# Opening of a transformer-like layer: scale and shift groups loaded by column quarters

## The chip, the cores and the metric

The kernel runs on one core of a Trainium2 chip. The metric is the device time of one execution in microseconds. The engines are TensorE (PE), VectorE (DVE), ScalarE (ACT), GpSimd (POOL) and SyncE (SP), which only issues DMAs here; ACT issues some too.

## The reference

One layer on 512 latent tokens and 256 context tokens of width 1024, all in fp32. A condition vector (c for the latents, c_ctx for the context) gives nine vectors of 1024 through one linear map, `ada_w` of 1024 x 9216: shift, scale and gate of three sub-layers. The opening computes groups 0 (shift) and 1 (scale) of these and the first sub-layer's h:

```python
ml = jnp.split((jax.nn.silu(c) @ ada_w[i] + ada_b[i])[:, None, :], N_MOD, axis=-1)
h = rms_norm(t, norm_g) * (1 + scale) + shift
x = t + gate * (0.5 * (silu(h @ w_gate) * (h @ w_up)) @ w_down)      # D_FF = 2816
```

Then follow a token mixer (an S5 scan branch and a gated linear attention branch) and a second FFN of the same form, on the latents alone.

## The kernel before

Activations lie transposed: h is eight tiles k of 128 features by 768 tokens. A product of fp32 matrices is made of three passes: h and each weight are split into a high part (rounded to fp32r) and a low part (the rest), and PE computes hi x lo, hi x hi and lo x hi. A weight unit is 128 columns of gate or up (512 KB, rows of 512 B); SP loads it into one of four raw slots, POOL splits it in `parts` (L1143 makes w_hi, L1146 w_lo). A job is one unit against all eight tiles of h, into a pair of PSUM banks; there are four pairs, and a job waits until its pair was read. FFN 1 starts with one segment of four tiles, that is jobs 0 to 7 (gate, up, gate, up, ...), and then eight down jobs. In it ACT makes silu of a gate job (L2241), DVE gates it with the up job (L3203), ACT makes act_hi (L2260) and DVE act_lo (L3206).

The engines run their own queues in the order written out by hand, tied by semaphores. Ahead of the jobs:

SP (L921 to L931) issues x (six tiles of 128 tokens), the eight tiles of `ada_w` of group 1 (scale, 128 rows of 1024 columns each, rows of 4 KB), unit 0, the eight of group 0 (shift), unit 1. They lie in memory that is free then: group 1 in w_hi and w_lo, group 0 mostly behind x in h's place. So POOL splits units 0 and 1 only once group 1 was multiplied (L1174), and units 2 and 3 once h is complete (L1176).

PE (L1258 to L1330) transposes the vectors and x feature tile by feature tile, each over all six token tiles; multiplies the columns of silu(c) and silu(c_ctx), padded to 32, with group 1 (`row_products`, L1280, four column strips at once, k added up in PSUM) and, between two halves of that, spreads the reciprocal roots over partitions (`spread_roots`, L1307); turns the row into columns (`turn_row`); does the same for group 0 with filler products between (`keep_busy`, L1290); turns lambda for the S5 branch. Then come jobs 0 and 1 together (L1499 to L1511): for each k both jobs' hi products, then both jobs' lo products (L1487, L1494), as the tiles of h come. From job 2 on a job runs by itself (L1244).

DVE (L3369 to L3406) copies x out of PSUM, takes the reciprocal, multiplies four tiles by the root (`plain_tile`), makes the scale (L2873, L2907), multiplies the other four by root and scale (`scaled_tile`), makes the shift, and makes h_lo in two pieces a tile (L3399). ACT scales the four plain tiles (L2163) and adds the shift on the way into h_hi (L2282). Behind that stand in DVE's queue: `s5_lambda`, the first two of eight tiles of ada group 2 (`ada_add`: L2857, L2860, two vectors each, products added up by DVE), `s5_angle` (13 small ops, L2728 to L2739) and then the gating of the FFN's tiles f = 0 to 3, with the other tiles of group 2 between them. In job 7 PE sums group 2's rows (L1366); it waits there (L1538) until all eight tiles were added:

```python
if n == 0:
    slot_free(js.down(2))
    pe.wait_ge(acc_ok, ada_added(ADA_START, KD))
```

Of the kernel before, what the change touches and what calls it, by code (L numbers as in the profile page):

```python
# [29 lines left out]
F32 = mybir.dt.float32  # L30
# [97 lines left out]
PLAIN = KD // 2  # L128
# [17 lines left out]
ADA_RING0, ADA_RING = 6, 2  # L146
ADA_EARLY = 4
# [37 lines left out]
JOINT_FROM = 2  # L185
# [12 lines left out]
UNIT, JOB = {}, {}  # L198

# [31 lines left out]
_number(JOB, [("vec", 1), ("x", KD), ("spread", 1), ("row1", 1), ("col1", 1), ("row0", 1), ("col0", 1), ("lam", 1), ("skip", 1),  # L231
# [156 lines left out]
def build(nc, a, out):  # L388
# [145 lines left out]
    ada_w0 = place("ada_w0", [P, ADA_RING0, D], F32, at=h_at + 24 * KB)  # L534
    ada_hi = place("ada_hi", [P, ADA_EARLY, D], F32, at=w_hi_at)
    ada_lo = place("ada_lo", [P, ADA_EARLY, D], F32, at=w_lo_at)
    ada_last = place("ada_last", [P, KD - ADA_RING0, D], F32, at=scratch_at + 24 * KB)
    squares = place("squares", [P, 6, D], F32, at=scratch_at)
    scaled = place("scaled", [P, KD, NT], F32, at=scratch_at)
    ada_row = place("ada_row", [P, 2, D // 4], F32, at=ada_at + 4 * ADA_RING * D)  # L540
    cs_wide = place("cs_wide", [P, KD, STRIP], F32, at=ada_at + 4 * ADA_RING * D + 4 * KB)
    assert scratch_at + 32 * KB <= s5_at

    def first_tile(g, k):

# [31 lines left out]
    s5t = place("s5t", [P, 16, DG], F32, at=s5t_at)  # L577
    lam_in = place("lam_in", [DG, 2, P], F32, at=s5t_at + 4 * KB)
# [145 lines left out]
    with ExitStack() as es:  # L724
# [28 lines left out]
        shift_ok = sem("shift_ok")  # L753
# [150 lines left out]
        def _(sp):  # L904
# [41 lines left out]
            def ffn(first, pre, parts, with_ada):  # L946
# [4 lines left out]
                def seg(part, i):  # L951
# [180 lines left out]
        def _(pool):  # L1132
# [97 lines left out]
        def _(pe):  # L1230
# [27 lines left out]
            pe.wait_ge(consts, 10)  # L1258
            pe.wait_ge(vec_in, 16 * 9)
            transpose(lat(JOB["vec"])[:, 0:P], vecs[:, :]).then_inc(job_done, 1)  # L1260

            for k in range(KD):
                j = JOB["x"] + k
                wait_read(pe, j)
                for t in range(6):
                    if k == 0:
                        pe.wait_ge(x_here[t], 16)
                    last = transpose((lat, ctx_)[t // 3](j)[:, P * (t % 3):P * (t % 3) + P], x_in[:, t, P * k:P * k + P])
                last.then_inc(job_done, 1)

            def row_products(g, k0=0, k1=KD):

                j = JOB[f"row{g}"]
                if k0 == 0:
                    wait_read(pe, j)
                for k in range(k0, k1):
                    pe.wait_ge(ada_here0[g][k], 16)
                    for q in range(4):
                        r = STRIP * q
                        last = pe.matmul(lat(j)[r:r + STRIP, 0:256], cs_wide[:, k, :], first_tile(g, k)[:, 256 * q:256 * q + 256],  # L1280
                                         start=(k == 0), stop=(k == KD - 1))
                    if k == KD - 1:
                        last.then_inc(job_done, 1)
                    if g == 0 and k < KD - 1:
                        keep_busy(2)

            def keep_busy(n):

                for _ in range(n):
                    pe.matmul(ctx_(JOB["row0"])[:, 0:P], ident[:, :], ident[:, :], start=True, stop=True)  # L1290

            def turn_row(g, jobs):

                j = JOB[f"col{g}"]
                wait_read(pe, j)
                for c in range(2):
                    last = transpose(lat(j)[:, P * c:P * c + P], ada_row[:, g, P * c:P * c + P])
                last.then_inc(job_done, jobs)
# [806 lines left out]
        def _(act):  # L2105
# [31 lines left out]
            for t in range(3):  # L2137
                row_squares(t)
# [1646 lines left out]
```

## Time and profile before

| | us |
|---|---|
| median of 3 runs | 1355.36 |
| lowest, highest | 1354.34, 1355.42 |
| span of the profiled execution | 1354.2 |
| PE busy in it | 1333.5 |
| DVE, POOL, ACT busy | 865.3, 651.0, 400.0 |

The span runs from the first to the last instruction; the median has the launch beside it. In the page's second part, 40 slices of 33.9 us, PE is at 9 tenths or more in all but the first, where it is at 5; that slice is the opening. Times in the views are us from the span's start, and lengths of groups are us busy. In a timeline an entry's length runs from its first instruction's start to its last one's end, and an instruction that had to wait for memory access shows the wait within its length.

### The profile page before, as it was taken

To read this page: it belongs to the slowest core of one execution; us is meant where nothing else is said; L and a number is where in the kernel's file an instruction comes from. 1 tells how busy PE (TensorE), PEld (TensorE's weight loads), DVE (VectorE), ACT (ScalarE), POOL (GpSimd) and SP (SyncE) were. 2 spreads that over 40 slices of the span, in tenths; PEclk is the share of its full clock that TensorE was granted. 3 is DMA by queue.
4 is the path that set the end of the run, shared out by engine and by line. 5 is a ranking of instruction groups with operands and counts; after the bars stand their busy time and mean duration, and the time that the engine had idled before them with its cause. 6 is when DMAs were issued, how large, how long until landed. Compare 5 with 4: busy or idle time off the path is not lost.

```text
span 1354.2 us, 21460 instructions
## 1 busy us (share of the span) xinstructions
PE 1333.5 (98%) x8546; PEld 1229.7 (91%) x8546; DVE 865.3 (64%) x1376; ACT 400.0 (30%) x757; POOL 651.0 (48%) x408
## 2 busy tenths in 40 slices
PE   5999999999999999999999999999999999999998
PEld 4899999999999999998888888888998999999997
DVE  5787368568556555437656649826778765555666
ACT  4320010210210110124635321222142555544455
POOL 1544444543543533532732356636467455655554
PEclk9999999999999999999999999999999999999999
DMA  9553354353444344223322479484736233344322
GB/s 357 161 148 85 121 148 120 120 157 116 126 135 139 102 126 158 62 55 109 80 62 52 126 212 259 152 266 148 229 87 199 63 94 94 107 115 114 101 72 85
DMA packets 236782, 178.18 MB, mean 132 GB/s; under 512 B 33416, under 2 KB 211852, under 8 KB 236684
## 3 DMA queue, kind: packets, MB, share of 16 engines
q1 hardware_dynamic: 216624, 145.78, 37.6%
q10 hardware_dynamic: 20060, 31.04, 7.0%
q8 instruction: 68, 1.11, 0.4%
q14 instruction: 30, 0.25, 0.1%
HBM read 156.93 MB, written 19.86 MB: 131 GB/s over the span
## 4 chain that ended last, share of the span: by engine, by line
PE 93%; DVE 3%; DMA 2%; SPq 1%; issue 1%; ACT 0%; DVEq 0%; ACTq 0%
PE ps L1244 47%; PE ps L1971 13%; PE ps L1566 13%; PE ps L2030 7%; DMA ada_w<-in_ada_w_dram 2%; PE ps L1255 1%; PE ps L1844 1%; DVE ada_acc L2860 1%; DVE ps L2972 1%; PE ps L2057 1%; PE ps L1881 1%; PE ps L1669 1%; PE ps L1487 1%; PE ps L1438 1%; PE ps L1706 1%
## 5 line engine op out<-in xcount | busy, mean ns | idle before, releaser
L1143 POOL TENSOR_SCALAR w_hi<-w_raw 128x1024 fp32r<-128x1024 f32 x128 | 153.4, 1198 | 527.8 <-PE ps L1244 276.0
L1146 POOL TENSOR_TENSOR w_lo<-w_raw,w_hi 128x1024 fp32r<-128x1024 f32 x128 | 325.4, 2542 | 10.7
L1244 PE MATMUL ps<-h_hi,w_lo 128*128 128x384 f32 (+2 forms) x1000 | 291.4, 351 | 0.0
L1244 PE MATMUL ps<-h_hi,w_hi 128*128 128x384 f32 (+2 forms) x1000 | 287.1, 346 | 0.0
L1244 PE MATMUL ps<-h_lo,w_hi 128*128 128x384 f32 (+2 forms) x1000 | 287.0, 346 | 0.0
L1244 PEld LDWEIGHTS ps<-h_hi,w_lo 128*128 128x128 f32 x1000 | 178.8, 188 | 14.9 <-issue 4.3
L1244 PEld LDWEIGHTS ps<-h_lo,w_hi 128*128 128x128 f32 x1000 | 180.6, 188 | 10.5
L1244 PEld LDWEIGHTS ps<-h_hi,w_hi 128*128 128x128 f32 x1000 | 180.4, 188 | 10.7
L1222 POOL TENSOR_TENSOR w_lo<-w_raw,w_hi 128x512 fp32r<-128x512 f32 x90 | 115.6, 1297 | 105.7 <-ACT w_hi L2609 104.2
L2860 DVE SCALAR_TENSOR_TENSOR ada_acc<-ada_w,cs,ada_acc 128x1024 f32<-128x1024 f32 x70 | 108.3, 1581 | 7.8 <-DMA ada_w<-in_ada_w_dram 5.5
L1971 PE MATMUL ps<-h_hi,w_hi 128*128 128x256 f32 x360 | 102.0, 283 | 0.0
L1971 PE MATMUL ps<-h_hi,w_lo 128*128 128x256 f32 x360 | 101.9, 283 | 0.0
L1971 PE MATMUL ps<-h_lo,w_hi 128*128 128x256 f32 x360 | 101.8, 283 | 0.0
L1566 PE MATMUL ps<-act_hi,w_lo 128*128 128x384 f32 (+1 forms) x352 | 94.6, 343 | 0.3 <-DVE x L3247 0.3
L1566 PE MATMUL ps<-act_lo,w_hi 128*128 128x384 f32 (+1 forms) x352 | 94.0, 341 | 0.0
L1566 PE MATMUL ps<-act_hi,w_hi 128*128 128x384 f32 (+1 forms) x352 | 94.0, 341 | 0.0
L2241 ACT ACTIVATE silu<-ps 128x768 f32<-128x768 f32 (+1 forms) x26 | 20.3, 781 | 198.6 <-PE ps L1244 190.9
L2260 ACT ACTIVATE act_hi<-ps 128x768 fp32r<-128x768 f32 (+2 forms) x26 | 20.0, 769 | 194.4 <-DVE ps L3203 194.4
L3245 DVE SCALAR_TENSOR_TENSOR x<-ps,mod,x 128x384 f32<-128x384 f32 (+2 forms) x120 | 49.1, 477 | 31.8 <-PE ps L1566 31.4
L1971 PEld LDWEIGHTS ps<-h_hi,w_lo 128*128 128x128 f32 x360 | 68.9, 191 | 0.3
L1971 PEld LDWEIGHTS ps<-h_lo,w_hi 128*128 128x128 f32 x360 | 68.7, 191 | 0.3
L1971 PEld LDWEIGHTS ps<-h_hi,w_hi 128*128 128x128 f32 x360 | 68.7, 191 | 0.0
(459 smaller groups left out, 2635.0 us busy)
## 6 DMA issues: line engine op xcount, KB each, us to landing
w_raw<-in_ffn_w_gate_dram SPq DMA_DIRECT2D x44, 512.0 KB, 5.1
w_raw<-in_ffn_w_up_dram SPq DMA_DIRECT2D x44, 512.0 KB, 4.1
w_raw<-in_ffn_w_down_dram SPq DMA_DIRECT2D x44, 512.0 KB, 4.5
ada_w<-in_ada_w_dram ACTq DMA_DIRECT2D x32, 512.0 KB, 3.9
w_raw<-in_w_in_dram SPq DMA_DIRECT2D x32, 512.0 KB, 4.3
ada_w<-in_ada_w_dram SPq DMA_DIRECT2D x30, 512.0 KB, 4.3
c_scr<-cp ACTq DMA_DIRECT2D x16, 288.0 KB, 3.8
b_scr<-bt_sb ACTq DMA_DIRECT2D x16, 256.0 KB, 3.9
```

Source lines behind the costliest of these rows:

```text
L1143: pool.tensor_scalar(w_hi[:, s, 0:cols], w_raw[:, s, 0:cols], 1.0, 1.0, ALU.mult, ALU.mult)\
L1146: pool.tensor_tensor(w_lo[:, s, 0:cols], w_raw[:, s, 0:cols], w_hi[:, s, 0:cols].bitcast(F32), ALU.subtract).then_inc(w_split, 1)
L1222: pool.tensor_tensor(lo, src, hi.bitcast(F32), ALU.subtract).then_inc(block_lo, 1)
L1244: last = pe.matmul(mv[2], st, mv[part], start=(first and q == 0), stop=(n == len(terms) - 1 and q == 2))
L1255: return pe.transpose(o, i, ident[0:i.shape[0], 0:i.shape[0]])
L1566: last = pe.matmul(bank, st[:, k, c], mv[:, k, cols], start=(k == 0 and r == 0), stop=(k == tiles - 1 and r == 2))
L1971: last = pe.matmul(bank_of(q, bank), st[:, k, :], mv[:, k, :], start=(opens and k == 0 and r == 0), stop=(closes and k == HK - 1 and r == ...
L2030: last = pe.matmul(ps[:, banks[e], :], st[:, k, c], mv[:, f + k, 0:NL], start=(k == 0 and r == 0), stop=(k == 1 and r == 2))
L2241: act.activation(dst, src, ACT.Silu).then_inc(slot_read[jg % 4], 1)
L2260: act.activation(dst, src, ACT.Copy).then_inc(act_hi_ok, 1)
L2860: STT(acc, tile, cs[:, k, v:v + 1], acc, ALU.mult, ALU.add).then_inc(acc_ok, 1)
L3245: ins = STT(x[:, k, c], src, mod[:, g, v:v + 1], x[:, k, c], ALU.mult, ALU.add)
```

## The change

Both groups are cut into four quarters of 256 columns, and a quarter of a group (1 MB, all 1024 rows, rows of 1 KB) is one DMA; two quarters (scale, shift) serve tiles 2q and 2q+1 of h. SP issues x, unit 0, quarter 0, units 1 and 2, quarters 1 and 2, and, once the rows of quarters 0 and 1 were made (`row_made`), quarter 3, which takes quarter 1's place; then unit 3 and so on. The memory of w_hi and w_lo stays free, so POOL waits for nothing but the load for units 0 to 3.

PE transposes x token tile by token tile, spreads the roots, makes quarter 0's rows and turns them. Then three jobs run together instead of two, and the products and turnings of quarters 1 to 3 and of lambda are written between their steps. Turning is four matmuls with two columns moving. DVE multiplies by the root five tiles ahead and three behind quarter 0; for each quarter it makes shift and scale in one op and the factor in another, scale-and-shift of two tiles in four ops on SBUF, and, after ACT has copied them into h_hi (one op a tile), two subtractions for h_lo. ACT's small loads (lambda, log_dt, gla_norm) move behind quarter 0. The cores of the new code:

```diff
+            first_unit(0)
+            quarter(0)
+            first_unit(1)
+            first_unit(2)
+            quarter(1)
+            quarter(2)
+            sp.wait_ge(row_made, 2)
+            quarter(3)
...
-                        if fresh and n < 4:
-                            is_done(pool, JOB["row1"])
-                            if n == 2:
-                                pool.wait_ge(h_ok, KD)
-                        else:
+                        if not fresh or n >= 4:
...
+            def row_products(q, g):
+
+                j = JOB["open"]
+                if g and q:
+                    pe.wait_ge(row_ok, q)
+                pe.wait_ge(ada_here0[g][q], 16)
+                for k in range(KD):
+                    r = STRIP * (k % 4)
+                    last = pe.matmul(lat(j)[r:r + STRIP, QW * g:QW * g + QW], cs_wide[:, k, :], quarter_tile(g, q)[:, k, :],
+                                     start=(k < 4), stop=(k >= 4))
+                if g == 0:
+                    last.then_inc(row_made, 1)
+
+            def turn_rows(q):
+
+                j = JOB["open"]
+                pe.wait_ge(row_ok, q + 1)
+                for g in range(2):
+                    for c in range(2):
+                        at = 8 * q + 4 * g + 2 * c
+                        last = pe.matmul(ctx_(j)[:, at:at + 2], ada_row[:, q % 2, QW * g + P * c:QW * g + P * c + P], strip_eye[:, 0:2],
+                                         start=True, stop=True)
+                last.then_inc(cols_made, 1)
...
+            row_products(0, 1)
+            keep_busy(6)
+            row_products(0, 0)
+            keep_busy(3)
+            turn_rows(0)
+            keep_busy(6)
...
+                    if joint:
+                        joint_start(0)
+                        joint_start(1)
+                        joint_step((0, 1), 0)
+                        joint_step((0, 1), 1)
+                        row_products(1, 1)
+                        row_products(1, 0)
+                        joint_start(2)
+                        joint_step((2,), 0)
+                        turn_rows(1)
+                        joint_step((2,), 1)
+                        joint_step((0, 1, 2), 2)
+                        row_products(2, 1)
+                        row_products(2, 0)
+                        joint_step((0, 1), 3)
+                        turn_rows(2)
+                        joint_step((2,), 3)
+                        joint_step((0, 1, 2), 4)
+                        row_products(3, 1)
+                        row_products(3, 0)
+                        joint_step((0,), 5)
+                        turn_rows(3)
+                        joint_step((1, 2), 5)
+                        joint_step((0, 1, 2), 6)
+                        turn_lambda()
+                        joint_step((0, 1, 2), 7)
...
+            for q in range(QUARTERS):
+                act.wait_ge(row_made, q + 1)
+                if q >= 2:
+                    act.wait_ge(cols_made, q - 1)
+                act.activation(ada_row[:, q % 2, :], lat(JOB["open"]), ACT.Copy).then_inc(row_ok, 1)
+                for k in (2 * q, 2 * q + 1):
+                    act.wait_ge(xn_ok, k + 1)
+                    act.activation(h_hi[:, k, :], scaled[:, k, :], ACT.Copy).then_inc(h_hi_ok, 1)
+                if q == 0:
+                    small_loads()
...
+            def quarter_mod(q):
+
+                c = slice(2 * q, 2 * q + 2)
+                dve.wait_ge(cols_made, q + 1)
+                by_group = mod[:, 0:2 * KD, :].rearrange("p (g k) v -> p g k v", g=2)[:, :, c, :]
+                bias = vt[:, 0:2 * KD].rearrange("p (g k) -> p g k", g=2)[:, :, c].unsqueeze(3).to_broadcast([P, 2, 2, 2])
+                link(TT(by_group, open_cols(q), bias, ALU.add))
+                last = STT(amul[:, 0, c, :], mod[:, KD + 2 * q:KD + 2 * q + 2, :], 1.0,
+                           vt[:, 72 + 2 * q:74 + 2 * q].unsqueeze(2).to_broadcast([P, 2, 2]), ALU.add, ALU.mult)
...
+                for k in (2 * q, 2 * q + 1):
+                    for t, v in ((slice(0, NL), 0), (slice(NL, NT), 1)):
+                        last = TS(scaled[:, k, t], scaled[:, k, t], amul[:, 0, k, v:v + 1], mod[:, k, v:v + 1], ALU.mult, ALU.add)
+                    last.then_inc(xn_ok, 1)
+
+            def quarter_low(q):
+
+                for k in (2 * q, 2 * q + 1):
+                    dve.wait_ge(h_hi_ok, k + 1)
+                    TT(h_lo[:, k, :], scaled[:, k, :], h_hi[:, k, :].bitcast(F32), ALU.subtract).then_inc(h_ok, 1)
...
             for k in range(PLAIN):
-                plain_tile(k, JOB["spread"])
...
+                plain_tile(k, j)
+            dve.wait_ge(silu_c, 2)
+            quarter_mod(0)
+            quarter_low(0)
             for k in range(PLAIN, KD):
-                scaled_tile(k, JOB["spread"])
...
+                last = plain_tile(k, j)
+            last.then_inc(slot_read[j % 4], 1)
+            for q in range(1, QUARTERS):
+                quarter_mod(q)
+                quarter_low(q)
```

The waits of the mixer's gate loads on reused semaphores (`gate_loaded`) count one DMA less for t of 4 and up.

## Rows read from the trace of the kernel before

**Rows 1.** Cores: span and mean granted clock of TensorE.

```profile
core 0: 1354.2 us, clock 0.998
```

**Rows 2.** The page, part 1: busy us, share of the span, instructions.

```profile
PE 1333.5 (98%) x8546; PEld 1229.7 (91%) x8546; DVE 865.3 (64%) x1376; ACT 400.0 (30%) x757; POOL 651.0 (48%) x408
```

**Rows 3.** Timeline, PE, opening: start, length, line, tiles, count [idle before].

```profile
18.45 1.93 PE L1280 MATMUL ps<-ada_hi,cs_wide 128*32 128x256 f32 x32 [0.38 <-issue]
...
27.23 0.64 PE L1280 MATMUL ps<-ada_w,cs_wide 128*32 128x256 f32 x8 [2.46 <-DMA ada_w<-in_ada_w_dram]
...
37.18 0.27 PE L1255 MATMUL ps<-ident,lam_in 64*128 64x64 f32 x1
...
37.53 0.27 PE L1255 MATMUL ps<-ident,lam_in 64*128 64x64 f32 x1
...
40.94 0.59 PE L1487 MATMUL ps<-h_hi,w_lo 128*128 128x384 f32 x2 [0.46 <-ACT h_hi L2282]
...
58.54 0.51 PE L1244 MATMUL ps<-h_hi,w_lo 128*128 128x384 f32 x2
...
102.57 0.28 PE L1366 MATMUL ps<-ones,ada_acc 128*128 128x1 f32 x2
```

**Rows 4.** Windows: PE, PEld, DVE, ACT, POOL busy; PEclk, DMA share, GB/s.

```profile
28.40:31.80 3.40, 3.40 (x22) 1.48 (x22) 2.53 (x7) 1.90 (x4) 0.00 (x0) 0.51 1.03 408
...
66.70:75.00 8.30, 8.30 (x49) 8.30 (x49) 6.91 (x10) 2.47 (x4) 3.51 (x2) 1.00 0.00 0
```

**Rows 5.** One line's view of L2857, then the timeline of DVE.

```profile
L2857 DVE TENSOR_SCALAR ada_acc<-ada_w,cs x2: 1527/2202/2878, 50.1 to 51.5; 128x1024 f32<-128x1024 f32 x2
...
50.07 4.33 DVE L2857 TENSOR_SCALAR ada_acc<-ada_w,cs 128x1024 f32<-128x1024 f32 x2
54.31 5.39 DVE L2860 SCALAR_TENSOR_TENSOR ada_acc<-ada_w,cs,ada_acc 128x1024 f32<-128x1024 f32 x2
...
60.86 2.29 DVE L2730 TENSOR_SCALAR s5t<-s5t 128x64 f32<-128x64 f32 x1
...
71.48 0.97 DVE L3203 SCALAR_TENSOR_TENSOR ps<-ps,silu 128x768 f32<-128x768 f32 x1
...
74.59 4.87 DVE L2860 SCALAR_TENSOR_TENSOR ada_acc<-ada_w,cs,ada_acc 128x1024 f32<-128x1024 f32 x4 [0.23 <-DVE act_lo L3206]
...
92.10 0.97 DVE L3203 SCALAR_TENSOR_TENSOR ps<-ps,silu 128x768 f32<-128x768 f32 x1 [0.76 <-PE ps L1244]
...
95.19 4.63 DVE L2860 SCALAR_TENSOR_TENSOR ada_acc<-ada_w,cs,ada_acc 128x1024 f32<-128x1024 f32 x2 [0.21 <-DVE act_lo L3206]
```

**Rows 6.** Timeline of POOL, splitting units 2 to 4.

```profile
51.13 2.71 POOL L1146 TENSOR_TENSOR w_lo<-w_raw,w_hi 128x1024 fp32r<-128x1024 f32 x1
...
60.70 2.40 POOL L1146 TENSOR_TENSOR w_lo<-w_raw,w_hi 128x1024 fp32r<-128x1024 f32 x1
63.06 1.05 POOL L1143 TENSOR_SCALAR w_hi<-w_raw 128x1024 fp32r<-128x1024 f32 x1
```

**Rows 7.** Lines by form and timeline, 18 to 50 us: ACT and DVE durations.

```profile
L2282 ACT ACTIVATE h_hi<-scaled,mod 128x512 fp32r<-128x512 f32 x8 | 5.7, 710 | 0.8 <-DVE mod L2873 0.8
...
L2156 ACT ACTIVATE ada_row<-ps 128x256 f32<-128x256 f32 x2 | 0.8, 383 | 12.6 <-PE ps L1280 12.6
...
22.05 3.55 DVE L3367 TENSOR_TENSOR scaled<-x,ps 128x768 f32<-128x768 f32 x4 [1.88 <-PE ps L1307]
```

**Rows 8.** DMA: packets in 24:32, 36.2:39.2, 92.3:95.5; issue to landing, L924, L918.

```profile
DMA packets 899, 3.25 MB, mean 406 GB/s; under 512 B 99, under 2 KB 111, under 8 KB 898
...
DMA packets 1705, 0.88 MB, mean 294 GB/s; under 512 B 18, under 2 KB 1703, under 8 KB 1704
...
DMA packets 1186, 1.18 MB, mean 368 GB/s; under 512 B 35, under 2 KB 1186, under 8 KB 1186
...
DMA to landing us min/median/max: 7.5/7.8/8.2
...
DMA to landing us min/median/max: 3.7/3.7/3.7
```

More of the change, by code:

```diff
@@ L1255, in transpose, with turn_x @@
                 return pe.transpose(o, i, ident[0:i.shape[0], 0:i.shape[0]])
[L1258 to L1263, printed above, removed]
+            def turn_x(t):
+                j = x_job(t)
                 wait_read(pe, j)
[L1265 to L1268, printed above, removed]
+                pe.wait_ge(x_here[t], 16)
+                for k in range(KD):
+                    last = transpose((lat, ctx_)[k // 4](j)[:, P * (k % 4):P * (k % 4) + P], x_in[:, t, P * k:P * k + P])
@@ L1269, in _, with turn_vecs @@
                 last.then_inc(job_done, 1)
[L1271 to L1285, printed above, removed]
+            def turn_vecs():
+                j = JOB["vec"]
+                wait_read(pe, j)
+                pe.wait_ge(vec_in, 16 * 9)
+                transpose(lat(j)[:, 0:P], vecs[:, :]).then_inc(job_done, 1)
@@ L1287, in keep_busy @@
             def keep_busy(n):
                 for _ in range(n):
[L1290 to L1298, printed above, removed]
+                    pe.matmul(ctx_(JOB["ffn1"])[:, 0:P], ident[:, :], ident[:, :], start=True, stop=True)
@@ L1479, in slot_free @@
                         pe.wait_ge(slot_read[j % 4], j // 4 + i * (part.jseg // 4))
-                    joint = 2 if two and part.segs + i == 0 else 0
+                    joint = JOINT if two and part.segs + i == 0 else 0
                     def joint_hi(v, k):
@@ L2151, in _ @@
             act.activation(root[:, :], root[:, :], ACT.Sqrt, bias=eps[:, :], scale=1.0 / D).then_inc(root_ok, 1)
-            for g in (1, 0):
-                j = JOB[f"row{g}"]
-                is_done(act, j)
-                act.activation(ada_row[:, g, :], lat(j)[:, 0:256], ACT.Copy).then_inc(slot_read[j % 4], 1)
-                was_read(act, j)
-                act.sem_inc(row_ok, 1)
-                if g == 1:
-                    act.wait_ge(cols_ok, 1)
-                    for k in range(PLAIN):
-                        for c, v in ((slice(0, NL), 0), (slice(NL, NT), 1)):
-                            ins = act.activation(scaled[:, k, c], scaled[:, k, c], ACT.Copy, scale=amul[:, 0, k, v:v + 1])
-                        ins.then_inc(xn_ok, 1)
+            j = JOB["vec"]
@@ L2276, in ffn @@
                         seg(part, i)
-            act.wait_ge(xn_ok, KD)
-            act.wait_ge(shift_ok, 1)
-            for k in range(KD):
-                for c, v in ((slice(0, NL), 0), (slice(NL, NT), 1)):
-                    ins = act.activation(h_hi[:, k, c], scaled[:, k, c], ACT.Identity, bias=mod[:, k, v:v + 1])
-                ins.then_inc(h_hi_ok, 1)
             for g in range(4):
@@ L3355, in norm_mixer @@
                         ALU.add, ALU.subtract).then_inc(hc_ok, 1)
-            def scaled_tile(k, j):
-                for b, c, v in ((0, slice(0, 384), 0), (1, slice(384, NL), 0), (1, slice(NL, NT), 1)):
-                    rs = both(j, 384)[:, b, c.start - 384 * b:c.stop - 384 * b]
-                    ins = STT(scaled[:, k, c], x[:, k, c], amul[:, 0, k, v:v + 1], rs, ALU.mult, ALU.mult)
-                ins.then_inc(xn_ok, 1)
             def plain_tile(k, j):
                 by_bank = [t[:, k, :].rearrange("p (b c) -> p b c", b=2) for t in (scaled, x)]
-                TT(by_bank[0], by_bank[1], both(j, 384), ALU.mult)
@@ L3395, in _ @@
-            dve.sem_inc(slot_read[j % 4], 1)
-            for k in range(KD):
-                dve.wait_ge(h_hi_ok, k + 1)
-                for c, v in ((slice(0, NL), 0), (slice(NL, NT), 1)):
-                    ins = STT(h_lo[:, k, c], scaled[:, k, c], mod[:, k, v:v + 1], h_hi[:, k, c].bitcast(F32),
-                              ALU.add, ALU.subtract)
-                ins.then_inc(h_ok, 1)
+                plain_tile(k, j)
+            dve.wait_ge(silu_c, 2)
+            quarter_mod(0)
+            quarter_low(0)
```

202 lines of the change are left out of this document (98 added, 104 removed).

## Prediction

> **What bounds the kernel now.** I read the core's span and clock first [rows 1], then the page's busy shares [rows 2]: one core, TensorE (PE) busy 98% of 1354.2 us. Outside the opening a change can only gain by starting PE's dense work earlier, and it loses by any stall put into it. So I read the opening in order of time, PE first [rows 3]. PE has nothing of the FFN until 40.94; before that stand x transposes, the row products of group 1 (scale; 1.93 us for four tiles of k, twice), a wait for the first tile of group 0 until 27.23, and group 0's products with filler. Jobs 0 and 1 end where L1244 first appears, 58.54 less the 0.17 of a started weight load: 58.4. From there one matmul pair costs 0.35 us, so a job of 24 pairs takes 8.3 us [rows 4], and "one tile-step" (one job, one k, three pairs) 1.04 us. Job 2 ends at 58.4 + 8.3 = 66.7. I call this time, when three jobs are done, T3: it is what the opening is worth. PE then runs without a gap to 102.57, where it starts the ada column sums in job 7; they wait for the last ada_acc of group 2. VectorE (DVE) ended that one at 95.19 + 4.63 = 99.8 [rows 5]. That slack of 2.75 us is the second thing to watch, because the change puts more DVE work between T3 and its start.
>
> **Two prices that the sum needs.** *DVE against POOL.* The two TENSOR_SCALARs of 128x1024 at L2857 took 1.53 and 2.88 us, the STT of 1024 at L2860 takes 1.22 when POOL is idle (4.87 for four) and 2.7 beside POOL (5.39 for two), and a 128x64 op of s5_angle took 2.29 beside w_lo [rows 5]. Set against POOL's rows [rows 6], each slow one ends just as a POOL instruction ends (the first TENSOR_SCALAR waits for w_hi's end, just before w_lo's start at 51.13, and ends at 50.07 + 1.53 = 51.60, so its own work is some 0.55; the second ends at 54.40, 0.55 behind w_lo's 51.13 + 2.71; 60.86 + 2.29 = 63.15 beside 63.10), and POOL's w_lo grows from 2.40 to 2.71 where it meets the first. They take turns, one whole instruction each: w_lo 2.40, w_hi 1.05. Ops with a PSUM operand I take to be free of it (L3203 reads PSUM and took 0.97 at 71.48 and at 92.10 alike; plain_tile 3.55 for four, 0.89 each [rows 7]). The Trainium skill, page "SBUF — State Buffer", section "SBUF: two separate sides", states this as an exclusive lock on a port pair, held for a whole instruction, against DVE ops with two SBUF inputs or in a 2-port mode; these rows agree, and it speaks against this change, which adds such ops exactly when POOL splits.
> *DMA.* 4 KB rows move at 406 GB/s (1.29 us for 512 KB), 512 B rows (a gate/up unit) at 294 (1.78), 1 KB rows at 368 (1.42) [rows 8]. A column quarter is 1 KB rows: 1.42, with 1.29 and 1.78 as its ends. The Trainium skill, page "DMA: Bandwidth & Descriptors", section "Specifications", gives 512 B as enough for line rate; the rows differ (294 against 406). By the page the first quarter would land some 1 us earlier and T3 fall by about as much.
>
> **The change, quarter 0.** x is unchanged and lands at 11.7 (3.48 + 8.2) [rows 8]. Turning by token tile lets PE and DVE follow the loads: eight transposes per tile and one copy of 1024 (1.2 us, from 0.89 for 768 elements of plain_tile, under the 1.4 between landings), so x is done near 14.1 instead of 20, the roots are spread by 16.0, five plain tiles by 20.5 (5 x 0.89). Unit 0 lands at 11.7 + 1.8 = 13.5; q0 at 13.5 + 4 x 1.42 = 19.1; unit 1 at 20.9, unit 2 at 22.7. PE: products of one group of a quarter 0.96 (half of 1.93), filler, done 20.4; row copy 0.6 (0.38 for half the width [rows 7]), turning 0.56 as for the three small transposes at 37.18; columns at 21.9. DVE: mod 0.2 (reads PSUM, free), then amul (two SBUF inputs) asks at 22.2. POOL's w_hi of unit 1 ran 21.0 to 22.05 and w_lo holds until 24.45. Turns follow: amul 24.6; w_hi of unit 2 to 25.7; scale-and-shift of 512 (0.3) to 26.0; w_lo to 28.4; the remaining three to 29.2. First h_hi (ACT, 768 wide, 0.95: between 0.71 for 512 and half as much again) 29.6, its h_lo 30.5. Without turns it would be 24.5; the price of the turns is 5 us. Were units 1 and 2 to come a little earlier or later, the end hardly moves, since four POOL instructions stand in the same 7 us.
>
> **The joint jobs on PE, summed from 29.6.** 24 tile-steps x 1.04 = 24.96; products of quarters 1 to 3, 3 x 1.93 = 5.79; three turnings x 0.56 = 1.68; lambda 0.56. Idle: PE runs out of ready tiles after each turning. Quarter 1: columns 37.3, h_hi of tile 2 at 37.3 + 0.5 (mod, amul) + 0.5 + 0.95 = 39.3 against PE at 38.3: 1.0. Quarter 2: quarter 3's loads are held until row_made reaches 2 (35.7), so unit 3 behind them lands 2.4 (the 3.7 from issue to landing less 1.29 [rows 8]) + 4 x 1.42 + 1.78 = 9.9 later, 45.6, and POOL splits it until 49.1. amul asks at 47.4: PE, free at 48.0, gets its tile at 50.7: 2.7. Quarter 3: nothing left on POOL, 0. T3 = 29.6 + 24.96 + 5.79 + 1.68 + 0.56 + 3.7 = **66.3**, against 66.7. So 11.3 us of earlier start (40.9 to 29.6) become 0.4: the same three jobs now have 8.0 us of products, turning and lambda inside them, which lay ahead of them before, and waits of 3.7 where they had 0.8.
>
> **Behind T3.** Quarter 3's low parts end near 61.5, lambda's turning at 63.2. In DVE's queue s5_lambda, four ada_add ops and s5_angle follow, then the gating of f=0. Before, this ran up to 71.48 from just ahead of 50.07, 17 us before T3; now it starts 3.1 us ahead. Step by step: lambda 0.6, two TENSOR_SCALARs 1.1 (POOL idle) to 64.8, STT 66.05, turn with w_hi of unit 4 (job 0 done 65.6), STT 68.35, then s5_angle's 13 small ops against w_lo of unit 4 and units 5 and 6 to 77.8, as they stood before against units 4, 5 and 6 (from 54.31 + 5.39 = 59.70 to 71.48, 11.8 us, with a free last one); that one and the gating at 78.5. From the gating to the last ada_acc it was 99.8 - 71.5 = 28.3, with 0.76 in it of DVE waiting for PE [rows 5], which falls away: 27.6. Last ada_acc at 78.5 + 27.6 = **106.1**. PE would be there at T3 + 35.9 = 102.2 and waits 3.9. Net 106.1 against 102.57: 3.6 us later. The slots of jobs 1 and 3 come free at about 81 and 93, wanted at 83 and 99.6: no stall. After it PE is bound again (s5_roots ends before job 7). The load waits of gates (gate_loaded) are hidden. Small loads move behind tile 1 on ACT's queue, which is free again well before the next row copy at 35.7, and are used only by lambda's turning: nothing waits.
>
> **Clock.** After its idle of 2.46 us [rows 3] PE was granted 0.51 for 3.4 us, the lower level, 1.2 GHz [rows 4]. The change has PE idle for some 3 to 5 us before 29.6 and 2.7 at 48: each half-speed stretch costs up to 1.7 us. The first may fall in a wait. I take 0 and keep 3.4 as the end.
>
> **Rivals.** *A, POOL and DVE miss each other in quarters 0 and 2*: against it, the 1.78 between q0's landing and unit 1's, shorter than the 2.9 that the columns need; for it, landings may stray. h starts at 25.0, idle 2.1: T3 = 25.0 + 24.96 + 8.03 + 2.1 = 60.1, last ada_acc 60.1 + 39.8 = 99.9: -2.7 us, 1352.7. If DVE's backlog also runs faster, PE's own time decides, T3 + 35.9 = 96.0: -6.6, 1348.8. This is the side not slower; it decides once T3 is under 62.8 (102.57 less 39.8, which is the last ada_acc less T3 in the forecast, 106.1 - 66.3). *B, the backlog is absorbed* (turns fall kindly behind T3, gating by 74.7): only T3 counts, -0.4, 1355.0. *C, the clock*: both stretches fall in dense work, +3.6 + 3.4 = +7.0, 1362.4. *D, it doesn't do what it says*: quarters land at 1.78 per 512 KB, q0 1.4 later and all behind it: +5.0, 1360.4; nothing later waits for DMA.
>
> **How the numbers follow.** The sum is made against the profiled 1354.2; the runs' median is 1355.36, 1.2 of it outside the span. Forecast: 1355.4 + 3.6 = **1359.0**. Chances: forecast 0.38, D 0.06, C 0.12 (slower, 0.56, of which 0.02 lie under the bound and count as same); B 0.14; A 0.30, of which 0.19 come out faster by over 0.2% and 0.11 within. 0.2% is 2.7 us, about what a measurement of this kernel can tell from no change. Faster 0.19, same 0.27, slower 0.54. Range: 1350.5 leaves out the far end of A, 1363 takes in C. The forecast's own range, with turns and rates at their ends, is 1357 to 1362.
>
> **What would show it.** Right: the first h_lo near 30, with amul or the scale-and-shift of quarter 0 lengthened to a POOL instruction's end; unit 3's split beside quarter 2; T3 near 66; gating of f=0 near 78; a PE stall of 2 to 5 us at L1366's new line, released by ada_acc. Wrong: h_lo at 25 to 26 and T3 near 60; or no stall at the sums. If quarters land later than 20 us, the DMA term was wrong; if the clock row shows 0.5 in the joint jobs, C.

## The result, and the profile after

The changed kernel takes **1371.66 us** (median of 4 runs, 1370.91 to 1374.1) against 1355.29 for the one before in the same comparison: ratio 1.0125, 95% interval 1.0111 to 1.014. It is 16.4 us slower. The forecast was 1359.0, its range ended at 1363.0. The sign was right, and so was the path up to the column sums in kind; what the forecast left at nothing is the price of TensorE's clock, in the opening and above all behind the stall. The profiled execution has a span of 1369.4 us, 15.2 more than before [rows 1].

The cores' view and part 1 of the page, changed kernel (compare [rows 1, 2]):

```profile
core 0: 1369.4 us, clock 0.989
...
PE 1345.8 (98%) x8566; PEld 1243.2 (91%) x8566; DVE 867.1 (63%) x1379; ACT 394.6 (29%) x743; POOL 646.5 (47%) x408
```

PE's share is 98% in both, yet its busy time grew by 12.3 us for 20 instructions more, and the clock fell from 0.998 to 0.989. Work that takes longer, not idle time, is the larger part of the loss. The timeline of PE says where:

```profile
29.17 0.65 PE L1522 MATMUL ps<-h_hi,w_lo 128*128 128x384 f32 x2 [4.68 <-ACT h_hi L2220]
...
38.12 0.95 PE L1328 MATMUL ps<-strip_eye,ada_row 128*128 128x2 f32 x8
38.92 0.60 PE L1522 MATMUL ps<-h_hi,w_lo 128*128 128x384 f32 x2
...
41.30 0.62 PE L1522 MATMUL ps<-h_hi,w_lo 128*128 128x384 f32 x2 [1.08 <-ACT h_hi L2220]
...
52.86 0.62 PE L1522 MATMUL ps<-h_hi,w_lo 128*128 128x384 f32 x2 [2.06 <-ACT h_hi L2220]
...
67.33 0.27 PE L1284 MATMUL ps<-ident,lam_in 64*128 64x64 f32 x1
...
71.14 0.51 PE L1273 MATMUL ps<-h_hi,w_lo 128*128 128x384 f32 x2
...
110.27 0.35 PE L1401 MATMUL ps<-ones,ada_acc 128*128 128x1 f32 x2 [3.26 <-DVE ada_acc L2912]
...
127.09 0.84 PE L1624 MATMUL ps<-act_hi,w_lo 128*128 128x384 f32 x2
```

The joint jobs start 11.8 us earlier than before (29.17 against 40.94), yet T3 is 71.14 less 0.17, 70.97, where it was 66.7. The column sums start at 110.27 behind a wait of 3.26 for the last ada_acc; before, they started at 102.57 without one [rows 3]. From there to the end of the span it was 1251.6 us before and is 1259.1 now: another 7.5 us go behind the stall, where the change touches nothing. One piece of work that both kernels share shows most of them, from the first column sum to the first down job (L1566 before, L1624 now). It took 112.09 - 102.57 = 9.5 us before and takes 127.09 - 110.27 = 16.8 now, 7.3 more. The first down job before:

```profile
112.09 0.50 PE L1566 MATMUL ps<-act_hi,w_lo 128*128 128x384 f32 x2
```

The windows (columns as in [rows 4]) show what they are, and two like them in the opening:

```profile
29.10:33.00 3.90, 3.83 (x13) 3.86 (x14) 3.90 (x5) 0.71 (x1) 0.00 (x0) 0.56 1.09 348
53.40:56.90 3.50, 3.50 (x13) 3.50 (x12) 1.27 (x2) 0.19 (x1) 0.00 (x0) 0.51 0.30 74
106.90:110.20 3.30, 0.11 (x1) 0.00 (x0) 3.30 (x5) 0.00 (x0) 2.32 (x2) 1.00 1.05 337
111.40:128.60 17.20, 17.20 (x65) 17.20 (x64) 10.49 (x15) 0.09 (x1) 8.74 (x7) 0.50 0.51 114
128.60:140.00 11.40, 11.40 (x67) 11.40 (x67) 9.98 (x31) 0.72 (x1) 2.39 (x1) 1.00 0.17 47
```

Row 3 is the stall. Row 4 follows it: PE is busy for all of 17.2 us, at 0.50, the lower level (1.2 GHz), and ends 65 matmuls, many of them of one column, where row 5 ends 67 of 384 columns in 11.4. Half of the 17.1 us at the lower level would be 8.5; the piece above shows 7.3, and 7.5 to the end of the span. The first two rows are the same thing in the opening, 3.4 us each, behind idle times of 4.68 and 2.06.

The changed kernel's timeline of DVE, in quarters 0 and 1 and behind T3, and then that of POOL in quarter 0:

```profile
23.35 1.19 DVE L3413 SCALAR_TENSOR_TENSOR amul<-mod,vt 128x4 f32<-128x4 f32 x1
24.58 4.35 DVE L3422 TENSOR_SCALAR scaled<-scaled,amul,mod 128x512 f32<-128x512 f32 x4
...
39.50 1.65 DVE L3422 TENSOR_SCALAR scaled<-scaled,amul,mod 128x512 f32<-128x512 f32 x4
...
72.84 2.41 DVE L2780 TENSOR_TENSOR s5t<-s5t 128x64 f32<-128x64 f32 x1
...
84.09 0.97 DVE L3247 SCALAR_TENSOR_TENSOR ps<-ps,silu 128x768 f32<-128x768 f32 x1
...
22.17 2.35 POOL L1179 TENSOR_TENSOR w_lo<-w_raw,w_hi 128x1024 fp32r<-128x1024 f32 x1
24.49 1.04 POOL L1176 TENSOR_SCALAR w_hi<-w_raw 128x1024 fp32r<-128x1024 f32 x1
25.61 2.38 POOL L1179 TENSOR_TENSOR w_lo<-w_raw,w_hi 128x1024 fp32r<-128x1024 f32 x1
```

The amul of four elements a partition waits for the end of w_lo (22.17 + 2.35 = 24.52), the four scaled instructions (0.41 each when POOL rests, the entry at 39.50) take 4.35 around w_hi and w_lo, as the turns in the prediction had it. Behind T3, s5_angle (twelve ops in both traces, not 13) takes from 72.84 to 84.05 beside the splits of units 4 to 6, and only then comes the gating of f = 0, 12.6 us later than before (71.48 in [rows 5]).

### The profile page after: what moved, and what is told of

Same layout as the page of the kernel before. It is cut to its first block, busy times and chain, and to the rows that moved or that the text cites. A ratio compares the mean times of both kernels' runs of the same rounds, so it can differ in the third digit from the quotient of the medians.

```text
span 1369.4 us, 21478 instructions
## 1 busy us (share of the span) xinstructions
PE 1345.8 (98%) x8566; PEld 1243.2 (91%) x8566; DVE 867.1 (63%) x1379; ACT 394.6 (29%) x743; POOL 646.5 (47%) x408
## 4 chain that ended last, share of the span: by engine, by line
PE 91%; DVE 6%; DMA 1%; issue 1%; ACT 1%; DVEq 0%
PE ps L1273 43%; PE ps L2029 13%; PE ps L1624 13%; PE ps L2088 7%; DVE ada_acc L2912 2%; PE ps L1284 2%; PE ps L1522 1%; PE ps L1902 1%; DMA ada_w<-in_ada_w_dram 1%; DVE ps L3016 1%; PE ps L2115 1%; PE ps L1939 1%; PE ps L1727 1%; PE ps L1473 1%; PE ps L1316 1%
## 5 line engine op out<-in xcount | busy, mean ns | idle before, releaser
L1179 POOL TENSOR_TENSOR w_lo<-w_raw,w_hi 128x1024 fp32r<-128x1024 f32 x128 | 323.2, 2525 | 10.7
L1624 PE MATMUL ps<-act_hi,w_lo 128*128 128x384 f32 (+1 forms) x352 | 94.9, 344 | 0.3 <-DVE x L3291 0.3
L1624 PE MATMUL ps<-act_lo,w_hi 128*128 128x384 f32 (+1 forms) x352 | 94.4, 342 | 0.0
L1624 PE MATMUL ps<-act_hi,w_hi 128*128 128x384 f32 (+1 forms) x352 | 94.1, 341 | 0.0
```

What stands on the lines that cost most here:

```text
L1179: pool.tensor_tensor(w_lo[:, s, 0:cols], w_raw[:, s, 0:cols], w_hi[:, s, 0:cols].bitcast(F32), ALU.subtract).then_inc(w_split, 1)
L1624: last = pe.matmul(bank, st[:, k, c], mv[:, k, cols], start=(k == 0 and r == 0), stop=(k == tiles - 1 and r == 2))
```

## Experiments

Two numbers sort them: when the column sums start, and the time from there to the end of the span. The second needs 1251 us where the clock stays up.

| kernel | median us | ratio to before, 95% | sums start | from there to the end |
|---|---|---|---|---|
| before | 1355.3 | | 102.57 | 1251.6 |
| after | 1371.7 | 1.0111 to 1.0140 | 110.27 | 1259.1 |
| e2_fill_stall | 1366.4 | 1.0068 to 1.0098 | 112.39 | 1252.6 |
| e5_load_order | 1368.4 | 1.0076 to 1.0110 | 107.34 | 1259.1 |
| e6_angle_early | 1360.9 | 1.0023 to 1.0053 | 108.04 | 1251.2 |
| e7_both | 1357.4 | 1.0004 to 1.0023 | 104.62 | 1251.0 |
| e10_best | 1353.6 | 0.9979 to 0.9996 | 101.03 | 1250.9 |
| e16_best_warm_wait | 1352.7 | 0.9976 to 0.9994 | 99.94 | 1251.0 |

### Is the slow stretch tied to the idle time?

**e2_fill_stall**, the changed kernel with identity matmuls under the stall:

```diff
     slot_free(js.down(2))
+    for _ in range(20):
+        pe.matmul(lat(js.down(2))[:, 0:P], ident[:, :], ident[:, :], start=True, stop=True)
     pe.wait_ge(acc_ok, ada_added(ADA_START, KD))
```

> The changed kernel, with 20 matmuls of 128x128 on the identity (0.157 us each, 3.1 us in all) just ahead of the wait for the last ada_acc, so that the 3.3 us stall stays in the time but TensorE is busy during it. Theory A (idle time is what lowers the clock behind it): the 17.1 us at 1.2 GHz vanish and the time is about 1371.7 - 8.5 = 1363. Rival B (the slow stretch is not tied to the idle time): 1371.7, with the 17 us at 1.2 GHz still there.

1366.4. Timeline of PE, then a window of the same kernel:

```profile
107.93 4.63 PE L1597 MATMUL ps<-ident 128*128 128x128 f32 x40
112.39 0.28 PE L1401 MATMUL ps<-ones,ada_acc 128*128 128x1 f32 x2
...
107.90:125.10 17.20, 17.20 (x127) 17.20 (x126) 15.79 (x20) 0.81 (x1) 14.05 (x8) 1.00 0.77 187
```

No idle time, no slow stretch: the 17.2 us that held 65 matmuls hold 127, 40 of them fillers. The sums start 2.1 us later than in the changed kernel, because a filler cost 0.23 us and not 0.157 and because T3 came at 72.05 in this execution, 1.1 later. The time still falls by 5.3. This carries the verdict: from the first sum to the first down job (121.91) it is 9.5 us again, so the 7.3 us were the clock. To the end of the span e2 is 6.5 of the 7.5 us better; the missing 1.0 lies behind PE's last matmul (6.2 us from there to the end, 4.6 in the kernel before).

**e1_sums_late** moves the wait instead, `n = 3 * (k - 5) + r`, with sums 2n and 2n + 1 in one slot.

> The changed kernel, with the column sums of adaLN group 2 begun nine matmul pairs later in job 7 (from k = 5 instead of k = 2) and made two at a time, so that TensorE reaches its wait for the last ada_acc about 3.1 us later and finds it nearly done (110.0 against 110.1 us). Theory A: the time lost behind the opening is a stall of 3.3 us at that wait, and the 17.1 us of TensorE at 1.2 GHz from 111.5 us on are a consequence of the stall; both go, 3.1 + 8.5 us, and the time is about 1360. Rival B: the slow stretch comes from something else (a fixed moment, or the half-speed stretches at 29.6 and 53.4 us, which stay); then only 3.1 us go, 1368.5. Theory A also expects that the half-speed stretches in the opening stay as they are.

1370.2, a miss for both. The wait at the sums shrank to 0.43, and PE then stood 6.30 us at the first down jobs, for the gating of f = 3. The clock fell 2.2 us into that wait and stayed at 1.2 GHz for 10.2 us, 6.1 of them behind the wait. Timelines of PE and of DVE:

```profile
111.08 0.58 PE L1401 MATMUL ps<-ones,ada_acc 128*128 128x1 f32 x4 [0.43 <-DVE ada_acc L2913]
...
126.06 1.01 PE L1625 MATMUL ps<-act_hi,w_lo 128*128 128x384 f32 x2 [6.30 <-DVE ps L3248]
...
120.22 0.97 DVE L2805 TENSOR_TENSOR s5t<-s5t 128x64 f32<-128x64 f32 x1
121.22 2.40 DVE L2806 TENSOR_TENSOR coef<-s5t 128x64 f32<-128x64 f32 x1
123.54 0.21 DVE L2807 TENSOR_TENSOR s5t<-s5t 128x64 f32<-128x64 f32 x1
```

DVE was still in s5_roots, whose small ops of 0.21 take 1.0 or 2.4 beside POOL's w_hi and w_lo. The backlog is a debt of DVE's queue: where PE doesn't wait for it at the sums, it waits at the next thing that DVE owes. In the changed kernel PE's own slowness behind the stall hid that second wait: there s5_roots was done at 121.2, and DVE waited for PE until 127.4.

**The stall put into the kernel before**, with a memset and 6 (e3) or 3 (e11) multiplies of a free buffer in DVE's queue ahead of the last ada_add, and with the 20 fillers of e2 (e4, e12):

```diff
+    if f_ == 2:
+        link(dve.memset(gu[:, 0, :], 0.0))
+        for _ in range(6):
+            link(TT(gu[:, 0, :], gu[:, 0, :], gu[:, 0, :], ALU.mult))
     for k in ((2, 3, 4), (5, 6), (7,), ())[f_]:
         ada_add(ADA_START, k)
```

> The kernel before, with one memset and six chained 128x768 multiplies of a buffer that is free (about 6.5 us) put into VectorE's queue ahead of the last ada_add, so that the last ada_acc comes at about 106.3 us and TensorE, which arrives at 102.6, waits 3.7 us. Nothing of the opening is touched. Theory A: the stall brings its own slow stretch, +3.7 and about +8.5, to 1367.5. Rival B: +3.7 us alone, 1359.0.

> As e3_before_stall, with the 20 identity matmuls (3.1 us) ahead of the wait. Theory A: only the stall itself is left, 1355.3 + 3.7 = 1359.0, and no stretch at 1.2 GHz behind it. Rival B (in which the delayed VectorE chain, not the clock, is what costs): the same time as e3_before_stall.

> The kernel before with half the delay of e3_before_stall: one memset and three 128x768 multiplies (0.7 + 3 x 2.2 us, as measured there beside GpSimd's splits) ahead of the last ada_add. The last ada_acc comes at about 106 us, TensorE waits about 3.5 us, as in the changed kernel. Theory: +3.5 us for the stall and +8.5 for some 17 us at 1.2 GHz behind it, 1367.3. Rival (only stalls of five us and more bring the slow stretch, and in the changed kernel it has another cause): 1358.8.

> As e11_before_3, with the 20 identity matmuls of e2_fill_stall (4.6 us) ahead of the wait, which now cover it whole: no idle time, no slow stretch, 1355.3 + 4.6 = 1359.9. Rival: the slow stretch comes all the same, 1368.

| | median us | idle at the sums | sums start | slow stretch | from there to the end |
|---|---|---|---|---|---|
| e3_before_stall | 1373.9 | 9.31 | 111.75 | 27.3 | 1260.4 |
| e4_before_stall_fill | 1374.6 | 4.77 | 111.15 | 20.5 | 1260.3 |
| e11_before_3 | 1371.2 | 6.24 | 108.61 | 20.5 | 1259.9 |
| e12_before_3_fill | 1370.3 | 1.77 | 109.04 | 17.1 | 1259.8 |

The size of the delay was wrong each time: six multiplies took 13.34 us beside POOL, not 6, so no filler covered the stall whole, and e4 and e12 say nothing of a covered one. Their times lie near the rivals' numbers, but with 4.77 and 1.77 us of idle time left that speaks for neither side. The slow stretch is counted from where the clock fell, which in e3, e4 and e11 was 7.3, 1.4 and 1.3 us before the wait ended; behind the wait PE ran slow for 20.0, 19.1, 19.2 and 17.1 us. What the four do say is firm: the kernel before, its opening untouched, loses 8.2 to 8.8 us behind a stall at this place, 1.8 us of idle time being enough (e12). So the loss behind the stall needs nothing else of the change.

```profile
102.64 4.63 PE L1539 MATMUL ps<-ident 128*128 128x128 f32 x40
109.04 0.38 PE L1366 MATMUL ps<-ones,ada_acc 128*128 128x1 f32 x2 [1.77 <-DVE ada_acc L2862]
...
110.40:127.40 17.00, 17.00 (x65) 17.00 (x64) 2.42 (x9) 0.19 (x1) 1.16 (x2) 0.50 0.08 19
```

(Timeline of PE and a window, e12_before_3_fill.)

### Why 17 us there, and 3.4 in the opening?

**e13_dense_first** keeps the wait at k = 2 of job 7 and makes the sums from k = 5 on, two a slot. **e14_sums_bunched** makes all 16 right behind the wait.

```diff
     pe.wait_ge(acc_ok, ada_added(ADA_START, KD))
-if 0 <= n < 2 * KD:
-    ada_sum(..., ADA_START, n)
+n -= 9                        # e13; e14: ada_sums(..., ADA_START) behind the wait
+if 0 <= n < KD:
+    ada_sum(..., ADA_START, 2 * n)
+    ada_sum(..., ADA_START, 2 * n + 1)
```

> The changed kernel with its wait for the last ada_acc where it is (k = 2 of job 7, a stall of 3.3 us), but the 16 column sums made only from k = 5 on, two at a time, so that nine pairs of 384-column matmuls follow the stall without a column sum between them. Theory S (what follows the stall sets how long the clock stays at 1.2 GHz, and the single-column matmuls between the others hold it there): the stretch is 3.4 to 10.2 us, as behind the opening's idle times and in e1_sums_late, in place of 17.1, and gives back half of the difference: 1371.7 - 3.4 to 6.8 = 1365 to 1368.3. Rival: a stall at this place costs 17 us at 1.2 GHz whatever follows, 1371.7.

> As the changed kernel, with all 16 column sums right behind the wait, one after the other (about 4 us), and plain 384-column matmuls behind them. Theory S: the column sums hold the clock low only while they run, so the stretch at 1.2 GHz is some 7 to 14 us and the time 1365 to 1370. Rival: 17 us, 1371.7.

1368.2 (1365.2 to 1371.2), at the upper end of theory S, and 1369.0. The stalls are as in the changed kernel, 3.29 and 3.33. Windows of e13, then the sums of e14 in the timeline and its windows:

```profile
112.70:116.10 3.40, 3.40 (x12) 3.40 (x11) 3.37 (x3) 0.00 (x0) 3.32 (x3) 0.50 0.40 54
116.10:129.00 12.90, 12.90 (x87) 12.90 (x87) 10.90 (x27) 0.81 (x1) 7.63 (x5) 1.00 0.68 166
...
110.78 5.98 PE L1394 MATMUL ps<-ones,ada_acc 128*128 128x1 f32 x32 [3.33 <-DVE ada_acc L2911]
...
116.60:122.00 5.40, 5.40 (x18) 5.40 (x19) 4.80 (x10) 0.00 (x0) 3.05 (x2) 0.50 0.61 140
122.10:130.00 7.90, 7.90 (x47) 7.90 (x47) 3.43 (x10) 0.81 (x1) 3.46 (x2) 1.00 0.50 122
```

With only 384-column matmuls behind the same stall, the clock is back after 3.4 us; with the single-column sums first, after 10.2; with a sum behind every pair, after 17.1 (111.5 to 128.5, where the sums last from 110.27 to 125.8). The sums that run later at full clock in e13 don't bring it down. So behind one and the same stall the length is set by what PE runs next. It isn't the only thing that counts: behind 2.06 us of idle time ahead of quarter 2's tiles the changed kernel had 3.4 us, behind 2.22 us at the same place e7_both had 6.8 (0.7 of them within the idle time), with the same work of PE behind. Nor do these runs show which property of the column sums holds the clock low. Both profiled executions have a further slow stretch of 3.4 us near 1052 us that the others lack; their medians are therefore less telling than the windows.

### What in the opening costs, and can it be had back?

**e5_load_order** loads unit 2 behind quarter 1 (`first_unit(2)` and `quarter(1)` exchanged). **e6_angle_early** turns lambda ahead of quarter 2's products, takes its exponential behind quarter 1's h_hi on ACT, and moves DVE's part:

```diff
     for q in range(1, QUARTERS):
         quarter_mod(q)
         quarter_low(q)
+        if q == 1:
+            s5_lambda()
+            s5_angle()
     dve.sem_inc(s5_in_used, 1)
-    s5_lambda()
     for k in range(2):
         ada_add(ADA_START, k)
-    s5_angle()
```

**e7_both** has both.

> The changed kernel, with weight unit 2 loaded after quarter 1 instead of ahead of it (order x, unit 0, quarter 0, unit 1, quarter 1, unit 2, quarter 2). GpSimd then has no split to do between 24.5 and about 30 us, so the amul of quarter 0 still waits for the end of unit 1's w_lo (24.5), but the four scaled instructions take 1.65 us and not 4.35. Theory (the turns that VectorE and GpSimd take at SBUF delay h by 2.7 us): first matmul of the joint jobs at about 26.4 instead of 29.2, job 2's end at about 68.1 instead of 71.0, and the time 1371.7 - 2.8 = 1368.9; the stall at the column sums and the 1.2 GHz stretch behind it stay. Rival: the opening is bound by something else (the landing of quarters 2 and 3, 36.6 and 45.9), the gain is lost again in idle ahead of quarters 2 or 3: 1371.7.

> The changed kernel, with the turn of lambda ahead of quarter 2's products, its exponential on ScalarE after quarter 1's h_hi, and s5_lambda and s5_angle (15 small instructions) in VectorE's idle time behind quarter 1 (43.1 to 49.7 us), where GpSimd has no split to do, instead of behind quarter 3. In the changed kernel they take 11.2 us there (72.84 to 84.05), seven of them over 0.9 us, beside GpSimd's splits. Theory A (the stall and the slow stretch come from VectorE's backlog behind the opening): gating of f = 0 at about 71.6 instead of 84.1, no wait at the sums, no 1.2 GHz behind them; 1371.7 - 3.3 - 7.5 = 1360.9. Rival B: the ada_adds, bound by the loads of the two ada_w buffers, or s5_roots in turns with GpSimd take the place of the angle, and a wait at the sums or at the first down steps (6.3 us in e1_sums_late) stays with its slow stretch: over 1366.

> Both edits, e5_load_order and e6_angle_early. If the two act apart: 1360.9 - 2.8 = 1358.1, job 2's end at 68.1 against 66.7 in the kernel before. Rival: without VectorE's backlog the earlier opening is worth less or more than alone; over 1360 or under 1356.

1368.42, 1360.94 and 1357.38: each within 0.8 us of theory. In e5 the scaled instructions fall from 4.35 to 1.65 us, the first matmul on h comes at 26.61, 2.6 earlier, and T3 at 67.7; the clock doesn't fall at the start of the joint jobs there, which is part of T3's 3.2. The stall (3.57) and its 17 slow us stay. In e6 the angle's twelve ops take 3.1 us (46.94 to 50.01) where they took 11.2 (five of them over 0.9 us), gating starts 11.4 us earlier, and neither the wait at the sums nor the slow stretch behind it is left. That e6 met its number to 0.1 is partly luck: its T3 came at 72.16, 1.2 later than in the changed kernel, with 5.7 us of idle time ahead of the joint jobs and 6.8 slow us where the changed kernel had 4.7 and 3.4. e2 and e13 show the same (T3 at 72.05 and 72.02), so one profile of this opening is good to about 1 us. Timelines: DVE in e5, DVE and PE in e6.

```profile
24.72 1.65 DVE L3422 TENSOR_SCALAR scaled<-scaled,amul,mod 128x512 f32<-128x512 f32 x4
...
46.94 0.23 DVE L2783 TENSOR_TENSOR s5t<-s5t 128x64 f32<-128x64 f32 x1
...
49.46 0.55 DVE L2794 RECIPROCAL s5t<-s5t 128x64 f32<-128x64 f32 x1
...
72.68 0.97 DVE L3250 SCALAR_TENSOR_TENSOR ps<-ps,silu 128x768 f32<-128x768 f32 x1 [1.18 <-ACT silu L2304]
...
108.04 0.28 PE L1403 MATMUL ps<-ones,ada_acc 128*128 128x1 f32 x2
```

**e8_warm_open** puts fillers into the opening of the changed kernel (`keep_busy(24)` for 6 ahead of the joint jobs, 8 identity matmuls ahead of quarter 2's tiles), **e9_both_fill_q2** nine ahead of quarter 2's tiles in e7.

> The changed kernel, with identity matmuls (0.23 us each, by e2_fill_stall) in the two longest idle times of TensorE in the opening: 18 more ahead of the joint jobs (4.1 us of the 4.7 idle) and 8 ahead of quarter 2's tiles (1.8 us of 2.1). Theory: the two stretches of 3.4 us at 1.2 GHz at 29.6 and 53.4 us go and give back up to 1.7 us each, 1371.7 - 3.4 = 1368.3, with the stall and the long slow stretch unchanged. Rival: the stretches stay or only shift, 1371.7, or the fillers run over and cost as much as they bring.

> e7_both with nine identity matmuls (0.23 us each, 2.1 us) in TensorE's 2.2 us of idle time ahead of quarter 2's tiles. In e7_both that idle time is followed by 6.8 us at 1.2 GHz (49.6 to 56.4 us). Theory: idle time lowers the clock, so the stretch goes and gives back half of it, 1357.4 - 3.4 = 1354.0, with the idle time itself still there under the fillers. Rival: the stretch stays or moves to another place, 1357.4.

e8: 1370.85 with runs from 1368.6 to 1372.5, not to be told from 1371.66; its profile has both slow stretches gone, T3 at 68.6 and the sums at 108.10, 2.2 earlier. e9: 1355.73, 1.7 under e7; the 6.8 slow us behind quarter 2's idle time are gone. The gain is half of the 3.4 expected, because 3.4 slow us came up at 27.5, at the start of the joint jobs, where e7 had none.

**e10_best** takes that idle time away:

```diff
-joint_step((0, 1), 3)
+joint_step((0,), 3)
 turn_rows(2)
-joint_step((2,), 3)
+joint_step((1, 2), 3)
@@ GpSimd, ahead of the split
+if fresh and n == 3:
+    pool.wait_ge(xn_ok, 6)
```

> e7_both, with the idle time ahead of quarter 2's tiles taken away instead of filled: turn_rows(2) goes ahead of jobs 1 and 2 of tile 3 (1.05 us earlier) and GpSimd splits unit 3 only after quarter 2's scaled tiles, so that amul takes 0.16 us and not 1.23. Idle 2.2 - 1.05 - 1.07 = 0.1 us; the 6.8 us at 1.2 GHz behind it go too: 1357.4 - 2.1 - 3.4 = 1351.9, below the kernel before (1355.3). Rival: only the idle time goes, or the stretch at 1.2 GHz alone, 1354 to 1355.3; or unit 3's later split delays the loads behind it, and the gain is lost: 1357.

1353.59, ratio 0.9988 (0.9979 to 0.9996): the first that is faster than the kernel before. T3 is 65.15. The missing 1.7 us to the expected value are a slow stretch at 27.6, behind the idle time ahead of the joint jobs. **e15_best_warm** and **e16_best_warm_wait** fill that one (`keep_busy(18)`); e15 as run lacks e10's GpSimd wait, e16 has it.

> e10_best with 12 more identity matmuls (0.23 us each, 2.8 us) in the 3.0 us of idle time ahead of the joint jobs. In e10_best 3.4 us at 1.2 GHz follow it (27.6 to 31.0 us). Theory: they go, 1353.6 - 1.7 = 1351.9. Rival: the stretch stays, or the fillers delay h's first matmul by as much: 1353.6.

> e10_best, its GpSimd wait ahead of unit 3's split included (e15_best_warm was sent without that wait, and unit 3's split took its turns with s5_angle and quarter 2 there), with 12 more identity matmuls ahead of the joint jobs. Theory: the 3.4 us at 1.2 GHz behind the opening's idle time go, 1353.6 - 1.7 = 1351.9, with job 2's end at about 63.6 instead of 65.3. Rival: the earlier row products only meet the landings of quarters 2 and 3 (37.1 and 43.1 us) or another wait, 1353.6.

1356.60, ratio 1.0009 (1.0000 to 1.0018), and **1352.74**, ratio 0.9985 (0.9976 to 0.9994). e16 stays 0.8 above its 1351.9; its T3 is 64.06 and its sums start 1.1 us earlier than in e10. The two kernels differ in one wait. Without it unit 3's split falls among s5_angle's last ops (DVE, e15), and PE waits 2.74 us for quarter 2; with it there is no such wait, and from the joint jobs to the last microsecond the clock doesn't fall (windows, e16):

```profile
44.25 1.07 DVE L2791 TENSOR_TENSOR s5t<-s5t 128x64 f32<-128x64 f32 x1
45.35 2.44 DVE L2792 TENSOR_TENSOR s5t<-s5t 128x64 f32<-128x64 f32 x1
...
27.10:40.00 12.90, 11.41 (x87) 9.87 (x88) 8.14 (x13) 4.02 (x5) 3.44 (x2) 1.00 1.09 329
40.00:64.00 24.00, 23.83 (x181) 20.69 (x180) 15.37 (x35) 6.40 (x10) 4.94 (x3) 1.00 0.52 145
```

## Why the prediction was right in kind and wrong in size

The step that failed is the clock term: the prediction took it as 0 in the opening, and "After it PE is bound again" gave the stall at the sums no price beyond its own length. The runs showed 7.3 to 7.5 us behind the stall and some 3 in the opening. The span grew by 15.2 us: 3.6 that were forecast, 4.1 more up to the sums, 7.5 behind them.

- **Loads, right.** q0 landed at 19.15 (forecast 19.1), unit 1 at 20.96 (20.9), unit 2 at 24.2 (22.7), q0's columns at 23.0 (21.9). The rate from 1 KB rows held. By the line rate of the Trainium skill's page "DMA: Bandwidth & Descriptors", section "Specifications", q0 would have come some 1 us earlier, an estimate; the measurement decides.
- **Turns of DVE and POOL, right.** First matmul on h at 29.17 (29.6), first h_lo at 30.0 (30.5). That unit 2 came 1.5 late and the columns 1.1 changed nothing, as the prediction said. The Trainium skill, page "SBUF — State Buffer", section "SBUF: two separate sides", holds here too (the later of the two instructions waits for the whole of the other): amul ends 0.02 behind w_lo. e5 gives the price of the turns with unit 2 alone: the first matmul on h comes 2.6 us earlier.
- **The joint jobs, wrong by 5.1, and T3 by 4.7.** From 29.17 to 70.97 are 41.8 us, forecast 36.7 from 29.6. Products came out at 5.6 (5.8), idle 3.1 (3.7), lambda 0.55. Turning took 0.81 of PE each, not 0.56: it was priced by three transposes, but is eight instructions in the trace, +0.75. In the two slow stretches a pair took 0.64 and not 0.35, which costs 1.6 of each 3.4 us, +3.1. That is rival C's end of the clock term, whose 0 was the choice that failed; the step said that the first stretch "may fall in a wait", and it began with the work (29.55). The rest, 2.1, is in the tile-steps, 24 priced at 1.04 by a job that runs alone.
- **Behind T3, right.** s5_lambda at 67.99, 3.0 ahead of T3 (3.1); gating at T3 + 13.1 (12.2); last ada_acc 26.0 behind it (27.6). T3's 4.7 late, gating's 0.9 more and 1.6 less from there make 4.0 of the 4.1. The stall was 3.26 for a forecast 3.9, since PE and DVE both came late. e6 shows the cause: s5_lambda's three small ops and s5_angle's twelve moved to where POOL rests, and the stall is gone.
- **Behind the stall, missed.** The clock step counted only the opening's idle times. Priced by [rows 4], even a stretch counted there would have been 1.7; it was 7.3 to 7.5, since the length depends on what follows, and column sums follow. e2, e12 and e13 show this term from three sides: filled, put into the kernel before, and shortened.
- **The sum.** With T3 at 71.0 and 7.5 behind the stall, the same steps give 1371.1 (71.0 + 12.2 + 27.6 = 110.8 for the last ada_acc, 8.2 behind 102.57, and 7.5, on 1355.4). No rival covered it: C had the opening's clock, none had a stall and the clock behind it together.
- **Rivals A and B.** Against A stood the landing times, and they held. B needed gating by 74.7; it came at 84.1.

## What to carry to other kernels

In this kernel a stall put into dense TensorE work cost twice: the wait, and the clock behind it, for a time that depended on what ran next; 3.3 us of wait brought 7.5 more. So look in the trace for what follows a stall, and price its slow stretch there. Two remedies worked here: fillers under the whole stall (e2), and nothing but large matmuls right behind it (e13). And before work is moved next to another engine's, look who takes turns with it then: twelve tiny VectorE ops cost 3 us alone and 11 beside GpSimd, and moving them, with s5_lambda and lambda's turning, took 10.7 of the 16.4 us back; with a load, a split and a turning moved as well, and fillers in one idle time, the kernel is 2.3 us under the one before.

## What the runs showed of the hardware that was not expected

- TensorE stayed at 1.2 GHz for 17 to 20 us although it was busy without a gap, as long as single-column matmuls stood between the large ones; with large ones alone it was back at 2.4 GHz after 3.4 us behind the same stall (e13), and 6.1 us behind the 6.30 us wait of e1_sums_late.
- The same length of idle time does not always lower the clock: 2.96 us ahead of the joint jobs did not in e7_both, 2.97 did in e10_best; 1.77 did in e12_before_3_fill, 1.86 did not in e5_load_order (24.8 us). What decides between them stays open here.
- Six multiplies of 128x768 in SBUF took 13.34 us beside GpSimd's splits (2.2 each), where a subtraction of that size took 0.91 with GpSimd at rest (two in 1.83 at 41.28, changed kernel). Up to 107.28 GpSimd ran three w_lo and two w_hi between them, and these grew too (w_lo to 2.96, w_hi to 1.77).
